# Ten of 22 up-projection pairs as seven block products, in a two-layer decoder step

## The reference

```python
def _causal_dwconv(z, prev, w_conv, b_conv):
    S = z.shape[1]
    ext = jnp.concatenate([prev, z], axis=1)
    out = b_conv + sum(ext[:, t:t + S] * w_conv[t] for t in range(CONV_W))
    return out, ext[:, -(CONV_W - 1):]
...
    h2 = _rmsnorm(x, lw['g_ffn']) * (1 + sc2) + sh2
    z, conv_new = _causal_dwconv(h2 @ lw['w_up'], conv_prev, lw['w_conv'], lw['b_conv'])
    zg, zv = z[..., :D_FF], z[..., D_FF:]
    x = x + g2 * ((jax.nn.silu(zg) * zv) @ lw['w_down'])
```

## Time and profile before

| | |
|---|---|
| median of 3 runs | 2257.74 us |
| the profiled execution | 2255.74 us |
| its span, first to last instruction | 2254.0 us |
| granted TensorE clock, mean | 0.997 of full |
| busy: PE, PEld | 98%, 88% of the span |
| busy: DVE, ACT, POOL | 52%, 39%, 29% |
| mean DMA traffic | 102 GB/s |

### The profile page before, as it was taken

The page is one execution under the profiler, slowest core; times in us unless marked ns, Lnnn a source line. Parts: engine busy times, 40 slices in busy tenths (PEclk is TensorE's granted clock), DMA queues, the critical chain, the costliest instruction groups (busy, mean ns, idle before and its releaser), DMA issues.

```text
span 2254.0 us, 42639 instructions
## 1 busy us (share of the span) xinstructions
PE 2210.7 (98%) x16239; PEld 1981.8 (88%) x16239; DVE 1170.6 (52%) x1831; ACT 874.9 (39%) x1815; POOL 655.1 (29%) x316
## 2 busy tenths in 40 slices
PE   7999999999999999999999999999999999999998
PEld 5899997667789999999988999966677999999998
DVE  4443753844346666651153717457443476666433
ACT  4223225832234555541132332366322355555322
POOL 0223433400022333333322334342000323333332
PEclk9999999999999999999999999999999999999999
DMA  9554332033333222235545333212332422222332
GB/s 302 170 145 100 85 85 66 19 109 108 85 130 91 79 84 84 84 109 167 173 126 176 83 97 83 79 43 63 97 108 57 156 70 83 79 80 83 87 85 84
DMA packets 338278, 230.69 MB, mean 102 GB/s; under 512 B 62732, under 2 KB 321605, under 8 KB 338140
## 3 DMA queue, kind: packets, MB, share of 16 engines
q1 hardware_dynamic: 336594, 226.37, 35.1%
q10 hardware_dynamic: 1546, 2.43, 0.4%
HBM read 223.15 MB, written 5.60 MB: 101 GB/s over the span
## 4 chain that ended last, share of the span: by engine, by line
PE 96%; DVE 2%; ACT 1%; DMA 0%; issue 0%; DVEq 0%; SPq 0%; ACTq 0%
PE PS L1550 62%; PE PS L1518 7%; PE PS L2000 5%; PE PS L2047 5%; PE PS L1912 3%; PE PS L1833 2%; PE PS L1646 2%; PE PS L1594 2%; PE PS L1936 2%; PE PS L1567 1%; PE PS L1889 1%; PE PS L1994 1%; PE PS L1950 1%; PE PS L2076 0%; DMA rows_in<-x_sample 0%
## 5 line engine op out<-in xcount | busy, mean ns | idle before, releaser
L975 POOL TENSOR_TENSOR wlo<-raw,whi 128x1024 fp32r<-128x1024 f32 (+1 forms) x248 | 586.0, 2363 | 1493.5 <-ACT whi L563 1493.5
L1550 PE MATMUL PS<-h_hi,whi 128*128 128x288 f32 x2496 | 740.7, 297 | 1.2 <-issue 1.0
L1550 PE MATMUL PS<-h_hi,wlo 128*128 128x288 f32 x2496 | 737.1, 295 | 0.0
L1550 PE MATMUL PS<-h_lo,whi 128*128 128x288 f32 x2496 | 737.0, 295 | 0.0
L563 ACT ACTIVATE whi<-raw 128x1024 fp32r<-128x1024 f32 (+1 forms) x252 | 258.4, 1025 | 919.6 <-PE PS L1550 823.5
L1550 PEld LDWEIGHTS PS<-h_hi,whi 128*128 128x128 f32 x2496 | 470.9, 189 | 9.4 <-issue 8.8
L1550 PEld LDWEIGHTS PS<-h_lo,whi 128*128 128x128 f32 x2496 | 471.0, 189 | 0.2
L1550 PEld LDWEIGHTS PS<-h_hi,wlo 128*128 128x128 f32 x2496 | 470.5, 188 | 0.0
L1452 DVE TENSOR_SCALAR conv<-zext,convp 128x592 f32<-128x592 f32 x88 | 153.6, 1746 | 132.5 <-ACTq L894 132.1
L1550 PE MATMUL PS<-act_hi,whi 128*128 128x288 f32 x704 | 209.9, 298 | 0.0
L1550 PE MATMUL PS<-act_hi,wlo 128*128 128x288 f32 x704 | 207.8, 295 | 0.0
(11 more groups left out here) (288 smaller groups left out, 3410.8 us busy)
## 6 DMA issues: line engine op xcount, KB each, us to landing
raw<-w_up SPq DMA_DIRECT2D x88, 512.0 KB, 3.8
pages<-cache_latent SPq DMA_DIRECT2D x256, 144.0 KB, 2.1
raw<-w_in SPq DMA_DIRECT2D x64, 512.0 KB, 4.0
ada_ring<-w_ada SPq DMA_DIRECT2D x41, 512.0 KB, 4.9
raw<-w_down SPq DMA_DIRECT2D x32, 512.0 KB, 3.9
ada_next<-w_ada SPq DMA_DIRECT2D x17, 512.0 KB, 4.0
ada_first<-w_ada SPq DMA_DIRECT2D x16, 512.0 KB, 10.4
raw<-w_out SPq DMA_DIRECT2D x16, 512.0 KB, 4.5
```

Of the source, the lines that this page charges most:

```text
L975: nc.gpsimd.tensor_tensor(wlo[:, slot, 0:n], raw[:, slot, 0:n], whi[:, slot, 0:n].bitcast(F32), ALU.subtract).then_inc(lo_ready.sem, 1)
L1550: r = mm(PS[0:m, 2 * (j % pairs) + half, 0:HT], w, o[:, k0 + k, half * HT:half * HT + HT], start=(first and k == 0 and part is whi and o i ...
```

## The change

The up stage alternates ordinary pairs (0, 1, 3, 5, ... 21: twelve) with **blocked** pairs (2, 4, ... 20: ten). A blocked pair is one product of a 256x1024 by a 1024x576 matrix, cut into 2x2 blocks of 128x512 and 512x288. Seven block products of sums of blocks replace eight: each product (`factor_products`) is 4 tiles k x 3 matmuls = 12 matmuls of 128x288. The seven products are told by their weights: A11, S2, S3, S1, A22, S4, A12, in the order in which PE makes them, into PS banks 0, 1, 2, 3, 0, 1, 2.

What it needs besides, in each layer:

- four sums of blocks of h (t1 to t4), once. ACT writes a full copy of h (`hf`, 8 more instructions in `high_parts`), POOL takes the four differences (`t_difference`, 128x1152), ACT their high parts, DVE the rests (`t_low`);
- for each blocked pair four sums of weight blocks on DVE (`weight_sums`, 128x512), high parts of all seven on ACT (`pair_hi_group`), the rest of six on POOL in three groups of 128x1024 (`pair_lo_group`; a group waits for its high part and for all four sums, whose place it overwrites) and the rest of A12 on DVE (`last_rest`);
- for each blocked pair the seven products are joined into the four quarters of the two tiles: ACT saves the first (`save_first`), DVE does U2, U3, C22 (three instructions), C21, C12 (two) and C11, each with one operand in PS.

Moved: the first tap goes from DVE to ACT (`first_tap`); the rests of ordinary units from POOL to DVE (`unit_rest`, written over `raw`); `act_hi` and `act_lo` of all 22 tiles are no longer made pair by pair but from pair 20 on (`act_split` on ACT, `act_rest` on DVE for 17 tiles and on POOL for 5), and the first output tile of the down stage waits for each tile k apart. Two steps of the next layer's conditioning that stood before the up stage go into the down stage. The rest is places in SBUF and shared semaphores.

The diff, cut to what the stages above do:

```diff
+FIRST, LAST = 2, KF - 2
+BLOCKED = range(FIRST, LAST + 1, 2)
+GROUPS = ((A11, S3), (S3, A22), (A22, A12), (A12, FACTORS))
+P_ORDER = (1, 6, 7, 5, 4, 3, 2)
+POOL_TILES = (6, 7, 9, 11, 15)
...
+                for p in BLOCKED[:-1]:
+                    sp.wait_ge(factor.sem, factor_done(l, p, 1))
+                    quarter(p + 2, a21[0][:], 1, 0, pair_in)
+                    quarter(p + 2, pair_w[:, A11], 0, 0, pair_in)
+                    sp.wait_ge(factor.sem, factor_done(l, p, 4))
+                    quarter(p + 2, pair_w[:, A22], 1, 1, pair_in)
+                    sp.wait_ge(factor.sem, factor_done(l, p, 2))
+                    quarter(p + 2, pair_w[:, A12], 0, 1, a12_in)
+                    up_unit(p + 3, 0)
+                    up_unit(p + 3, 1)
...
+                for p in BLOCKED:
+                    if p > FIRST:
+                        evacuated(p - 1, 1)
+                    save_first(p)
+                    history(p, 0)
+                    act.wait_ge(zconv.sem, tile_half(zconv, l, p - 1, 1))
+                    history(p, 1)
+                    hi(l, up_unit_of(p + 1, 1), 0, 1)
+                    act.wait_ge(joined.sem, join_done(l, p, C21))
+                    first_tap(p, 1)
+                    act.wait_ge(joined.sem, join_done(l, p, C11))
+                    first_tap(p, 0)
+                    if p < LAST:
+                        pair_hi_group(p + 2, 0)
+                        pair_hi_group(p + 2, 1)
+                        silu(p)
+                        pair_hi_group(p + 2, 2)
...
+                    evacuated(p + 1, 0)
+                    if p < LAST:
+                        pair_hi_group(p + 2, 3)
+                        hi(l, up_unit_of(p + 3, 0), 0, 0)
...
+                    silu(p + 1)
...
+                for p in BLOCKED:
+                    for g in range(3):
+                        pair_lo_group(p, g)
...
+                def other_taps(j, s):
+
+                    f = j + KF * s
+                    c = conv[s][:, 0:ZE - 2]
+                    dve.wait_ge(tap0.sem, tile_half(tap0, l, j, s))
+                    v.scalar_tensor_tensor(c, zext[:, s, 1:ZE - 1], convp[:, 0, f + 2 * KF:f + 2 * KF + 1], c, ALU.mult, ALU.add)
+                    v.drain()
+                    v.scalar_tensor_tensor(c, zext[:, s, 0:ZE - 2], convp[:, 0, f:f + 1], c, ALU.mult, ALU.add).then_inc(zconv.sem, 1)
...
+                for p in BLOCKED:
+                    other_taps(p - 1, 1)
+                    join_u2(p)
+                    product(p - 1)
+                    join_u3(p)
+                    join_c22(p)
+                    if p == LAST:
+                        unit_rest(p + 1, 0)
+                    unit_rest(p + 1, 1)
+                    join_c21(p)
+                    join_c12(p)
+                    other_taps(p, 1)
+                    join_c11(p)
+                    if p < LAST:
+                        weight_sums(p + 2)
+                    other_taps(p, 0)
...
+                    product(p)
+                    if p < LAST:
+                        last_rest(p + 2)
...
+                    other_taps(p + 1, 0)
+                    if p < LAST - 2:
+                        unit_rest(p + 3, 0)
...
-                dense(l, "up", U_UP, 44, KD, h_hi, h_lo, first=2)
...
+                for p in BLOCKED:
+                    group_ready(p, 0)
+                    if p > FIRST:
+                        pe.wait_ge(joined.sem, join_done(l, p - 2, C11))
+                    factor_products(p, A11, *b11, 0)
...
+                    factor_products(p, S2, *sum2, 1)
+                    group_ready(p, 1)
+                    factor_products(p, S3, *sum3, 2)
...
+                    factor_products(p, S1, *sum1, 3)
+                    group_ready(p, 2)
+                    pe.wait_ge(saved.sem, saved.at(l, blocked(p) + 1))
+                    factor_products(p, A22, *sum4, 0)
+                    pe.wait_ge(joined.sem, join_done(l, p, U2))
+                    factor_products(p, S4, *b22, 1)
+                    pe.wait_ge(last_low.sem, last_low.at(l, blocked(p) + 1))
+                    pe.wait_ge(joined.sem, join_done(l, p, U3))
+                    factor_products(p, A12, *b21, 2)
+                    for s in range(2):
+                        use(l, up_unit_of(p + 1, s))
+                        pe.wait_ge(tap0.sem, tile_half(tap0, l, p - 1, s))
+                        products(s, KD, h_hi, h_lo, 0, 2 + s, pairs=4, low=wlo if p == LAST else raw_lo).then_inc(unit_used.sem, 1)
```

More of the change, by code:

```diff
@@ L508, in _, with up_unit @@
                             conditioning(l, n)
[L509 to L517, removed]
+                def up_unit(j, s):
+                    u = up_unit_of(j, s)
+                    if j > FIRST + 1:
+                        sp.wait_ge(unit_used.sem, unit_used.at(l, u - 1))
+                    unit(l, u, s, raw[:, s].rearrange("p (k n) -> p k n", k=8),
+                         A["w_up"][l, :, DF * s + 128 * j:DF * s + 128 * j + 128].rearrange("(k p) n -> p k n", p=128))
@@ L1541, in weights, with products @@
                 return part[:, slot, m * k:m * k + m]
-            def products(slot, nk, xh, xl, k0, j, first=True, last=True, m=128, pairs=2):
+            def products(slot, nk, xh, xl, k0, j, first=True, last=True, m=128, pairs=2, low=wlo):
                 for half in range(2):
                     for k in range(nk):
-                        for part, operands in ((whi, (xh, xl)), (wlo, (xh,))):
+                        for part, operands in ((whi, (xh, xl)), (low, (xh,))):
                             w = weights(part, slot, k, m)
@@ L1550, in products @@
                                 r = mm(PS[0:m, 2 * (j % pairs) + half, 0:HT], w, o[:, k0 + k, half * HT:half * HT + HT],
-                                       start=(first and k == 0 and part is whi and o is xh), stop=(last and k == nk - 1 and part is wlo))
+                                       start=(first and k == 0 and part is whi and o is xh), stop=(last and k == nk - 1 and part is low))
                 return r
@@ L2110, in _, with factor_products @@
                 ada_turn(l, 5, ada_rows)
-                dense(l, "up", U_UP, 44, KD, h_hi, h_lo, first=2)
+                use(l, U_UP + 2)
+                products(0, KD, h_hi, h_lo, 0, 2, pairs=4).then_inc(unit_used.sem, 1)
+                use(l, U_UP + 3)
+                pe.wait_ge(mod_ev.sem, mod_ev.at(l, 6))
+                products(1, KD, h_hi, h_lo, 0, 3, pairs=4).then_inc(unit_used.sem, 1)
+                def factor_products(p, q, hi_of, lo_of, bank):
+                    for k in range(KD // 2):
+                        for part, operands in ((pair_hi, (hi_of, lo_of)), (pair_lo, (hi_of,))):
+                            for o in operands:
+                                r = mm(PS[:, bank, 0:HT], part[:, q, 128 * k:128 * k + 128], o[k],
+                                       start=k == 0 and part is pair_hi and o is hi_of, stop=k == KD // 2 - 1 and part is not pair_hi)
+                    r.then_inc(factor.sem, 1)
```

524 lines of the change are left out of this document (366 added, 158 removed).

## The result

The changed kernel takes 2337.98 us (median of 4 runs, 2336.94 to 2338.46) where the kernel before takes 2257.53: a ratio of 1.0359, 95% interval 1.0346 to 1.0371. It is slower by 80 us, 21 more than forecast; the time lies two microseconds from the first rival's 2340. The profiled execution took 2336.94 us.

What follows compares the result with a forecast made beforehand. PE bounds the kernel before (busy 98% of the span). Per layer -15.9 + 11 + 25.6 + 10 = +30.7, twice +61.4, on the profiled 2255.7: 2317 us, range 2285 to 2345.

Steps and rivals of the forecast that it cites:

- the first rival: In the turns, POOL is served in order of request: ring 28.0 us, 9 x 1.3 more per layer, 2340 us; chance 0.13.
- a ring of DVE and ACT: Per turn (blocked plus ordinary pair), a DVE-ACT chain back to its start takes 26.7 us against PE's 23.9; PE waits 2.8.
- step 9: Last ring step: ACT silu, high parts, evacuation, tap, then `last_rest`: 4.7 us, plus 1.5 from POOL's groups, not entering the product.
- 120 matmuls less: Ten blocked pairs per layer with 84 matmuls instead of 96, at 132.7 ns each: -15.9 us a layer.
- start: Start of up stage: DVE and POOL work one after the other until pair 2's fourth product: +11 us a layer.
- nine turns: Up stage: eight turns with PE waiting 2.8 us, the last 3.2: +25.6 us a layer.
- end: End of up stage: taps, rests and products on DVE and POOL in line make the last rest late: +10 us a layer.
- moved conditioning steps: Two conditioning steps moved from before the up stage into the down stage: the same matmuls elsewhere, taken at no cost.
- steps 1 to 8: Ring parts before step 9: DVE taps, joins, sums and ACT evacuations, 1.2 to 4.4 us each; POOL's first group delays the final tap.
- At nothing: Things taken to cost nothing: weight loads, the two moved conditioning steps, and ACT's 8 extra copies of 0.6 us each.
- One group costs: In each turn only one POOL group costs, the others fall into waits: ring 25.2 us, 2269 us; chance 0.09.
- faster: POOL's groups run beside joins or ACT's stretches; below 2.6 us of blocking a turn PE's 23.9 bounds: 2230 us; chance 0.18.

Runs made afterwards that it cites:

- the swap at the start: In the changed kernel, DVE makes the rest of the third unit ahead of the first pair's four weight sums; 2338.42 us.

## Why the prediction was right, and where a term was off

The direction and the mechanism held: a ring of DVE and ACT, made longer than PE's 23.9 us by POOL's three groups, with PE waiting for the save. The four experiments on the turn came out as that account says, and the one that removes only POOL's width removes the whole wait. One step of it, the order in which POOL and DVE are served in step 9, was wrong. The range, 2285 to 2345, took in the ring of either order, so that the time lies inside it says nothing for the order that was chosen. The terms, for layer 0, from the rows and the starts of PE's matmuls:

| term | forecast | measured |
|---|---|---|
| 120 matmuls less | -15.9 | -15.9 |
| start | +11 | +11.5 |
| nine turns | +25.6 | +31.9 |
| end | +10 | +12 |
| moved conditioning steps | 0 | +1 |
| sum | +30.7 | +40.5 |

The measured terms are distances between starts of PE's matmuls (711.84, 783.69, 1003.56, 1024.64, 1188.21) less the matmuls in them at 132.7 ns and less the same distances before. Twice 40.5 is 81.0; the profiled executions differ by 81.2.

**The saving** is exact: 132.2 ns a matmul in unbroken turns. The 122.5 ns worked out from the Trainium skill's formula ("TensorE: Matmul & The Clock Gate", Back-to-back issue gap), which the page gives for an isolated matmul and not for a stream, is met by no run here.

**The ring, steps 1 to 8.** In the trace of after they take 1.73, 2.70, 1.74, 4.39, 1.20, 1.74, 3.15 and 3.71 us; the sum forecast 1.74, 2.7, 1.74, 4.4, 1.2, 1.74, 3.15 and 1.74 + 2.1. Each is within 0.15 us, all priced from rows of before; with step 9 the parts come to 27.6, 0.1 more than the ring, since two of the ends overlap the next start. Only ACT's first tap, taken as 0.70 like silu, took 0.87.

**Step 9 is the step that failed**: 7.2 us instead of 4.7 + 1.5. The prediction held that POOL's third group couldn't come between the product's two instructions, and took the earlier trace rows as the reason: a DVE instruction in an undrained run had gone first although POOL had asked. It did come between (856.1, with DVE's 64 columns at 856.66), and the product ended at 859.07. So the order of service was the wrong step and the only large one. The trace of before already had the same thing, in rows that the prediction doesn't show. DVE, then POOL:

```profile
284.98 1.23 DVE L1253 TENSOR_TENSOR y_lo<-win,y_hi 128x1024 fp32r<-128x1024 f32 x1
...
286.12 2.42 DVE L1253 TENSOR_TENSOR y_lo<-win,y_hi 128x64 fp32r<-128x64 f32 x1
...
285.09 3.38 POOL L975 TENSOR_TENSOR wlo<-raw,whi 128x1024 fp32r<-128x1024 f32 x1 [2.89 <-ACT whi L563]
```

No drain stands between the two DVE instructions, POOL asked during the first, and the 64 columns behind it took 2.42 us instead of 0.22: the product's row to a hundredth. Five places of this kind in the trace of before, undrained and with both operands in SBUF, go this way, and only the earlier trace rows the other. What the earlier trace rows shows fits the same order too, if DVE's instruction had asked before 1172.45, while the one ahead of it still ran; no run shows when it asked. In the product POOL's third group could ask when the second ended, 856.1. That DVE's 64 columns asked later, near the end of the 512, is inferred from the order and not seen.

The run with the third group held back makes the assumed order true by a wait: turn 26.19, total 2315.8, where the forecast with this assumption was 26.7 and 2317. That the totals agree so closely is partly luck: the turn is 0.5 us shorter than forecast, 9 us in 18 turns, and what start, end and the moved steps cost above the forecast (the table: 3.5 us a layer) makes up 7 of them.

The Trainium skill's rule ("SBUF — State Buffer", Who interferes with whom: whoever issues first has the shared ports for its whole instruction) is what the runs show, and with it the first rival's ring of 28.0; it missed by 0.6, 0.3 of it in step 9 (7.5 against 7.2). That rival had 0.13. One row was weighed against one row and a rule, and the row that was taken had a second reading.

**The start**, mis-sized by little, and for the right reason as far as the runs show: it is a sum of DVE and POOL work up to one point. The fourth product of pair 2 starts at 754.67, forecast 755.4. POOL's first difference (716.39) holds an `h_lo` of the norm (2.50 us instead of 0.75), its second and third hold two of the weight sums (3.01 and 3.12 us instead of 0.69), and behind these stands the rest of the third unit, for which PE waits 4.4 us. The forecast hadn't named that wait, and the swap at the start shows that it cost nothing by itself. Of the 11.5, 1.7 are lower clock behind that wait, which wasn't in the forecast.

**The turns**: 3.14 us in the first, then 27.48 - 23.89 = 3.6 in each of eight (27.43 or 27.44 in most, 27.8 in one), forecast 2.8. As forecast, PE waits for the save; the wait alone looks smaller than the loss (1.8), because the clock hides the other half.

**The end**: 3.6 us up to the first down matmul and 9.5 in the down stage, less the 1 us of the moved steps. POOL's weight rests stood in the sum, but among the signs only the wait for act_lo was named; in the changed kernel PE waits for either alike (6.6 and 6.5 us), and moving the weight rests gave the more. Where the turns have no backlog, the part up to the first down matmul nearly disappears: the runs with the groups cut or on DVE begin the down stage at 988 and 990 us instead of 1024.6, some 3 us earlier than nine shorter turns explain, and need 163 us for it as the changed kernel does.

**At nothing** was right for the loads: in the 210 us of turns of the version with the groups on DVE PE has no gap. It was right for ACT's copies: DVE goes from tile to tile of the norm in 1.32 us before and after, but for the one `h_lo` that POOL holds. The two conditioning steps were not at nothing. Before, 16 of their matmuls filled the time in front of the first product of the stage, and PE waited 0.18 us for `h_lo`; now it waits 1.04 there, and their work stands in the down stage:

```profile
711.09 1.05 PE L1646 MATMUL PS<-ada_ahead,cond 128*32 128x256 f32 x16
712.32 0.37 PE L1594 MATMUL PS<-h_hi,whi 128*128 128x288 f32 x1 [0.18 <-DVE h_lo L1087]
```
```profile
711.84 0.37 PE L1897 MATMUL PS<-h_hi,whi 128*128 128x288 f32 x1 [1.04 <-DVE h_lo L1292]
```

(The first is the kernel before.) Work that fills a wait is not free to move.

**The rivals.** "One group costs" (2269) and "faster" (2230) fall for the kernel as it is: all three groups cost. But the faster case named its place and its price correctly: below 2.6 us of blocking a turn PE's 23.9 bounds. The groups on DVE pass that point, and with start and end relieved as well the kernel takes 2240, 10 us from the 2230 that was worked out. What still lies between wasn't taken apart further; the waits shown last, at the two ends of the stage, come to 6.1 us in layer 0, where the 2230 allowed 3.

## What to carry to other kernels

DVE with two SBUF operands and POOL are one resource, not two: add up their times, and give work to POOL only where DVE reads PS or waits (line 1264 took 0.82 us in all 16 cases, 8 of them beside a POOL rest). Here a rest costs 2.4 us on POOL and holds DVE meanwhile, and 1.15 on DVE. Ask of every short instruction on the path what may be asked for ahead of it; a wait on the other engine that keeps it from standing in front can be worth more than the work it delays. Where a ring sets the time, measure its period from start to start, since PE's waits understate the loss by what the lower clock takes.

## What the runs showed of the hardware that was not expected

- A DVE instruction of 64 columns (0.22 us) took 2.41 us directly behind a DVE instruction on which it didn't wait, because POOL had asked in between. No drain is needed for that; line 1253 in the kernel before shows the same, 2.42 us.
- POOL's group of 1024 columns, 2.40 us alone, took 2.85 beside one DVE instruction each; halves took 1.3 to 1.8. The third group of the run that holds it back, with no DVE instruction beside it but the last rest, took 2.40 again: the longer duration is waiting, not a lower rate.
- PE's clock fell to the lower level behind waits of 1.8 us already, in 14 of the 18 turns: 24 stretches in the execution against 4 before. It is not sure to fall: it did so in 6 of 18 turns with the third group held back (waits of 0.6 to 2.0 us) and in 1 of 18 with the groups halved (1.7 us in most). In the turns without a wait it stayed at 1.00.
- Seven block products in groups of 12 matmuls, with semaphores between, run at 132.2 ns a matmul, as the ordinary pairs do.
